# RWKV chunk matrices kept as 64 columns, with products on 64x64 tiles and grams of the diagonal blocks alone

## What is computed

```python
def step(state, inp):
    r_t, d_t, k_t, v_t, kk_t, a_t = inp
    s_a = jnp.einsum('bhvk,bhk->bhv', state, -kk_t)
    state = (state * d_t[:, :, None, :] + s_a[..., None] * (kk_t * a_t)[:, :, None, :]
             + v_t[..., None] * k_t[:, :, None, :])
    return state, jnp.einsum('bhvk,bhk->bhv', state, r_t)
wkv, y = lax.scan(step, wkv0, (rh, dh, kh, vh, kk, ah))
```

## Time and profile before

| | |
|---|---|
| median of 3 runs | 1603.11 us (1602.9 to 1606.72) |
| the profiled execution | 1596.52 us, span 1594.9 us, mean granted TensorE clock 0.972 |
| TensorE products | 1497.1 us busy (94%), 7652 records |
| TensorE weight loads | 784.4 us (49%) |
| VectorE | 585.6 us (37%), 963 instructions |
| ScalarE | 270.2 us (17%) |
| GpSimd (POOL) | 137.2 us (9%) |
| chain that ended last | TensorE 61%, DMA 30%, issue 4%, VectorE 3%, ScalarE 2% |

### The profile page before, as it was taken

How to read it: one execution, slowest core, us unless ns; L and a number is a source line. 1 busy time by engine, 2 the same in 40 slices (tenths; PEclk the granted TensorE clock), 3 DMA queues, 4 the chain that set the end, 5 groups by cost and what they waited for, 6 DMA issues and landing times.

```text
span 1594.9 us, 20792 instructions
## 1 busy us (share of the span) xinstructions
PE 1497.1 (94%) x7652; PEld 784.4 (49%) x7652; DVE 585.6 (37%) x963; ACT 270.2 (17%) x535; POOL 137.2 (9%) x256
## 2 busy tenths in 40 slices
PE   8999989799899888899999999999999999999995
PEld 6877545467788764443344344344334334334431
DVE  2999846823455544312112122121221221211214
ACT  1111523222211112110111111011011011011102
POOL 5332332130110020000000000000000000000000
PEclk9999999899899989899999999999999999999998
DMA  9899997793011063699999999999999999999994
GB/s 337 332 342 345 375 361 253 267 307 118 15 54 53 1 241 122 266 418 429 429 429 428 428 429 429 428 430 428 428 428 429 429 429 427 429 428 429 429 428 188
DMA packets 67886, 534.13 MB, mean 335 GB/s; under 512 B 8587, under 2 KB 9686, under 8 KB 35062
## 3 DMA queue, kind: packets, MB, share of 16 engines
q1 hardware_dynamic: 48774, 471.52, 71.6%
q0 software_dynamic: 8656, 41.97, 7.3%
q10 hardware_dynamic: 10400, 19.92, 3.4%
HBM read 528.92 MB, written 4.46 MB: 334 GB/s over the span
## 4 chain that ended last, share of the span: by engine, by line
PE 61%; DMA 30%; issue 4%; DVE 3%; ACT 2%; POOL 0%; POOLq 0%; SPq 0%; DVEq 0%; ACTq 0%
PE bank L786 58%; DMA projT<-in_w_gate_up 26%; PE bank L787 2%; DMA ring<-in_w_mem_kv 1%; DMA ring<-in_w_in 1%; DMA arena<-in_state_rw_wkv 1%; DMA out_wkv_sample<-arena 1%; ACT arena L1618 0%; DMA ring<-in_cache_sb_v 0%; DVE arena L2288 0%; DMA arena<-in_x_sample 0%; POOLq L459 0%; DVE arena L2377 0%; DVE arena L2394 0%; ACT memT L1889 0%
## 5 line engine op out<-in xcount | busy, mean ns | idle before, releaser
L786 PE MATMUL bank<-arena 128*128 128x128 f32 (+7 forms) x2130 | 326.7, 356 | 12.5 <-DVE arena L2337 3.6
L786 PE MATMUL bank<-ring,memT 128*64 128x512 f32 (+2 forms) x1152 | 283.8, 600 | 10.8 <-ACT memT L1889 8.3
L786 PEld LDWEIGHTS bank<-arena 128*128 128x128 f32 (+4 forms) x2130 | 221.3, 179 | 126.4 <-issue 112.5
L786 PE MATMUL bank<-projT,ring 128*128 128x264 f32 x1056 | 260.1, 402 | 7.5 <-DVE projT L2297 2.7
L2501 DVE TENSOR_SCALAR arena<-bank 128x256 f32<-128x256 f32 x64 | 27.0, 421 | 639.2 <-PE bank L786 639.2
L786 PE MATMUL bank<-projT 128*64 128x512 f32 (+1 forms) x1056 | 232.4, 586 | 9.1 <-DMA projT<-in_w_gate_up 9.1
L786 PE MATMUL bank<-ring,projT 128*64 128x512 f32 x1024 | 230.3, 597 | 0.0
L786 PEld LDWEIGHTS bank<-projT,ring 128*128 128x128 f32 x1056 | 204.1, 198 | 49.9 <-issue 5.2
L786 PEld LDWEIGHTS bank<-ring,memT 128*64 128x64 f32 (+2 forms) x1152 | 85.0, 139 | 156.8 <-issue 138.0
L786 PEld LDWEIGHTS bank<-projT 128*64 128x64 f32 (+1 forms) x1056 | 75.1, 138 | 161.7 <-issue 134.9
L786 PEld LDWEIGHTS bank<-ring,projT 128*64 128x64 f32 x1024 | 69.3, 137 | 147.4 <-issue 147.4
(11 more groups left out here) (272 smaller groups left out, 853.1 us busy)
## 6 DMA issues: line engine op xcount, KB each, us to landing
ring<-in_w_gate_up SPq DMA_DIRECT2D x64, 2048.0 KB, 22.0
projT<-in_w_gate_up SPq DMA_DIRECT2D x64, 2048.0 KB, 24.3
ring<-in_w_down SPq DMA_DIRECT2D x64, 2048.0 KB, 20.4
ring<-in_cache_sb_k SPq DMA_DIRECT2D x64, 256.0 KB, 6.2
ring<-in_cache_sb_k POOLq DMA_DIRECT2D x64, 256.0 KB, 5.9
ring<-in_cache_sb_v SPq DMA_DIRECT2D x64, 256.0 KB, 5.6
ring<-in_cache_sb_v POOLq DMA_DIRECT2D x64, 256.0 KB, 5.4
ring<-in_w_in ACTq DMA_DIRECT2D x7, 2048.0 KB, 14.0
```

Source lines behind the costliest of these rows:

```text
L786: mm = lambda out, l, r, first, last, **k: pe.matmul(out, l, r, start=first, stop=last, **k)
```

## The change

- The matrices of a unit keep 64 columns: partitions 0 to 63 hold chunk 0's block, partitions 64 to 127 chunk 1's. The masks have 64 columns too.
- X, TX, XT, MV and Z become `in_chunks`: eight products of 64x64 tiles with 64 moving columns, one on rows and columns 0 to 63, one on 64 to 127, in turn.
- `grams` takes both head halves together, and only the diagonal blocks: 64x64 tiles on all four positions, into two banks. All of g2 now stands ahead of dS(1).
- RB, RK and the inverse for WT stay 128 wide, block diagonal: RB and RK are zeroed once by POOL (new wait `blocks_zero`), `Tfull` by VectorE, and only their diagonal blocks are written. In level 4 VectorE writes `Tl` (64 columns, for Z) and then `Tfull` in two halves (for WT). Z now waits for `T_last`, not for the bank of XT4.
- VectorE's and ScalarE's operations on these matrices have half the columns; those on RB and RK are twice as many, on 64 partitions each.

```diff
-        lev = [sb(f"lev{i}", [P, P]) for i in range(6)]
+        lev = [sb(f"lev{i}", [P, C]) for i in range(6)]
...
-                g.tensor_tensor(lev[i][:], same[i + 1], lo, ALU.subtract).then_inc(sem("masks"), 1)
-            link(g.tensor_tensor(m_up[:], tri_lt[:], blk[:], ALU.mult))
...
+                for h in halves:
+                    ins = g.tensor_tensor(lev[i][h, :], same[i + 1][h, h], lo[h, h], ALU.subtract)
+                ins.then_inc(sem("masks"), 1)
+            for h in halves:
+                link(g.tensor_tensor(m_up[h, :], tri_lt[h, h], blk[h, h], ALU.mult))
...
+            g.wait_ge(*full_of(("ys", 0)))
+            for a in RBs + RKs:
+                ins = g.memset(a, 0.0)
+            ins.then_inc(sem("blocks_zero"), 1)
             g.wait_ge(sem("out_done"), 16 * n_out)
             g.sem_inc(sem("arena_clear"), 1)
...
+            def grams(n, nm):
...
+                bs = [start((nm, hp) + n) for hp in range(2)]
                 for i, lr in enumerate({"g1": ("BA", "AB"), "g2": ("BR", "KA"), "g3": ("KR",)}[nm]):
                     for tl in range(2):
...
+                        for hp in range(2):
+                            rows = slice(64 * hp, 64 * hp + 64)
+                            for cc, h in enumerate(halves):
+                                cols = slice(tt * P + C * cc, tt * P + C * cc + C)
+                                ins = mm(bs[hp][h, P * i + C * tl:P * i + C * tl + C], hats[lr[0]][rows, 2 * hh + tl, cols],
+                                         hats[lr[1]][rows, 2 * hh + tl, cols], True, True)
...
+            def in_chunks(b, left, right):
+
+                for u in range(4):
+                    for h in halves:
+                        last = mm(b[h, C * u:C * u + C], left(u)[h], right(u)[h], True, True)
+                return last
...
-                    for u in range(4):
-                        last = mm(b[:, u * P:u * P + P], Nm[lv % 2][:, u, :], Tm[:, u, :], True, True)
-                    done(("X", lv) + n, last)
+                    done(("X", lv) + n, in_chunks(b, lambda u: Nm[lv % 2][:, u, :], lambda u: Tm[:, u, :]))
...
+                pe.wait_ge(sem("T_last"), it + 1)
+                b = start(("Z",) + n)
+                done(("Z",) + n, in_chunks(b, lambda j: Tl[:, 2 * (j % 2) + j // 2, :], lambda j: MVs[:, j, :]))
                 gone(pe, ("XT", 4) + n)
...
-                        last = mm(b[64 * hp:64 * hp + 64, P * tl:P * tl + P], tokAB[:, 0, c0:c0 + 64], Tt[:, u, :], True, True)
+                        last = mm(b[64 * hp:64 * hp + 64, P * tl:P * tl + P], tokAB[:, 0, c0:c0 + 64], Tfull[:, u, :], True, True)
...
                 if ahead:
-                    gram(ahead, "g2", 0)
+                    grams(ahead, "g2")
                 state_change(1)
-                if ahead:
-                    gram(ahead, "g2", 1)
...
-                    move(("X", lv) + n, Xm.rearrange("p a b -> p (a b)"), lambda b: b[:, :])
+                    move(("X", lv) + n, Xm.rearrange("p a b -> p (a b)"), lambda b: b[:, 0:256])
...
             v.wait_ge(sem("arena_clear"), 2)
+            v.memset(Tfull, 0.0)
             v.memset(Sb[0], 0.0).then_inc(sem("S_zero"), 1)
...
-                    tt_(RBs[it % 2][:, u], part(b, 0), m2(m_upi), ALU.mult)
+                    for h in halves:
+                        tt_(RBs[it % 2][h, u, h], part(b, 0)[h], m2(m_upi)[h], ALU.mult)
...
+                if it == 0:
+                    v.wait_ge(sem("blocks_zero"), 1)
                 other_products(it)
...
-                    tt_(Tt, Tt, b[:, :].rearrange("p (a b) -> p a b", a=4), ALU.add).then_inc(freed_by(("XT", lv) + n), 1)
+                    if lv < 4:
+                        tt_(Tt, Tt, units(b), ALU.add).then_inc(freed_by(("XT", lv) + n), 1)
+                    else:
+                        tt_(Tl, Tt, units(b), ALU.add).then_inc(sem("T_last"), 1)
+                        for h in halves:
+                            ins = tt_(Tfull[h, :, h], Tt[h], units(b)[h], ALU.add)
+                        ins.then_inc(freed_by(("XT", lv) + n), 1)
```

More of the change, by code:

```diff
@@ L343, in build @@
         tokABs, tokKVs = ([ar(R0 + 1024 * i + 512 * j, 2, 256) for i in range(2)] for j in range(2))
-        Nt, Tm, Tt, Xm, AK = (ar(R0 + 2048 + 512 * i, 4, P) for i in range(5))
+        Nt, Tm, Tt, Xm, AK, Tl = (ar(R0 + (2048, 2304, 2560, 2816, 3072, 3840)[i], 4, C) for i in range(6))
+        Tfull = ar(R0 + 3328, 4, P)
         RBs, RKs = ([ar(R0 + 4608 + 1024 * i + 512 * j, 4, P) for i in range(2)] for j in range(2))
-        Nm = [ar(R0 + 6656 + 512 * i, 4, P) for i in range(2)]
+        Nm = [ar(R0 + 6656 + 512 * i, 4, C) for i in range(2)]
+        last_state = ar(R0 + 6656, 4, P)
         MVs, Zs, Us = (ar(R0 + 7680 + 256 * i, 4, 64) for i in range(3))
@@ L376, in build @@
         moe_slot = [ring[:, 0, :], ring[:, 2, :], proj[:, 0:SLOT], proj[:, SLOT:2 * SLOT], ring[:, 3, :], ring[:, 1, :]]
+        halves = (slice(0, C), slice(C, P))
         gate_at = lambda dt: pT[:, (V0 if dt < 4 else K0 - 4) + dt, :]
@@ L1198, in turned_hats @@
                 done((nm,) + n, last)
[L1200 removed]
+            def grams(n, nm):
                 tt, hh = n
[L1203 to L1205 removed]
+                bs = [start((nm, hp) + n) for hp in range(2)]
                 for i, lr in enumerate({"g1": ("BA", "AB"), "g2": ("BR", "KA"), "g3": ("KR",)}[nm]):
                     for tl in range(2):
[L1208 to L1210 removed]
+                        last = []
+                        for hp in range(2):
[4 more added lines that the diff above has]
+                                         hats[lr[1]][rows, 2 * hh + tl, cols], True, True)
+                            last.append(ins)
+                for hp in range(2):
+                    done((nm, hp) + n, last[hp])
+            def in_chunks(b, left, right):
[3 more added lines that the diff above has]
+                return last
             def group_mean(t):
@@ L1228, in _ @@
             for nm in ("g1", "g2"):
-                for hp in range(2):
-                    gram(RW_PARTS[0], nm, hp)
+                grams(RW_PARTS[0], nm)
             for it, n in enumerate(RW_PARTS):
@@ L1234, in _ @@
                 tokAB, tokKV, RB, RK = (x[it % 2] for x in (tokABs, tokKVs, RBs, RKs))
-                for hp in range(2):
-                    gram(n, "g3", hp)
+                grams(n, "g3")
                 branches(*at_place(it, "start"))
```

54 lines of the change are left out of this document (21 added, 33 removed).

## The result

The changed kernel took 1584.72 us (median of four runs, 1578.9 to 1589.78) against 1603.01 for the kernel before (1598.1 to 1606.72): ratio 0.9887, 95% interval 0.9843 to 0.993. A second set of six runs gave 1581.68 against 1598.92, ratio 0.9873 (0.9836 to 0.9911). It is faster, by 17 to 18 us. The forecast was 1580, a saving of 23.3, with a range of its own of 1574 to 1586.

The account below looks back on a forecast made before the run. TensorE bounds the RWKV stage, DMA the expert stream behind it. Savings of 13.9 (levels), 3.5 and 0.1 (their end), 4.9 (grams) and 0.9 (start) sum to 23.3: 1603.1 to 1579.8 us; own range 1574 to 1586, wider range to 1600.

Parts of the forecast that it names:

- Level: One level of the RWKV stage: 2.93 us instead of 3.80, held by TensorE's products and branches; 0.87 saved.
- The step that counted four whole levels a part: RWKV stage: 0.87 us saved a level, taken for 16 levels over four parts, 13.9 us.
- End of the levels: From the first X4 record to the branches behind WT: 5.01 us instead of 6.16, 1.15 saved; 3.5 in three parts.
- Grams and transition: Between parts: Y starts 1.35 us sooner and g3 saves 0.27, together 1.62 three times, 4.9 us.
- A part: Period of one of the four parts of the RWKV stage: down from 36.4 to 30.1 us.
- The start: First part's grams and VectorE's first masks shrink while the clock is at half: 0.9 us saved, between 0 and 3.
- The fourth part: End of the last part's levels: 0.7 us gain up to XT4 cut by 0.6 more on VectorE, leaving 0.1.
- POOL: Memsets hidden behind a 10.15 us DMA; perhaps 1.5 us more mask work hidden in 3.45 us idle: no cost.
- The rule that spoke against it: X, TX and XT pairs: row tiles can't share a PSUM bank simultaneously; held strictly, tiles run in turn, 1614 us.
- whatever moves the start of the experts moves the end one for one: Behind the RWKV stage: experts wait for every layer ahead, so the whole 23.3 us saving was subtracted from the end time.
- The third rival: TensorE's clock falls inside the RWKV stage: four half-clock levels cost 7.5 us, so 1587; all sixteen near 1611; chance 0.08.
- The expert stream unchanged in length: Expert weights' DMA stream, from 646 us to the end: a sign that its length stays the same.

Follow-up runs that it names:

- the two kernels with the code of before: The unedited kernel before, and the same with five more POOL mask operations (ratio 1.0004): 1052.2 and 1052.4 us from first reciprocal to end.
- The kernel with 13 products: Changed kernel, last eight branch products moved into TensorE's wait in the last part, 13 unread products added before the rank counts: 1572.74 us, ratio 0.9816.
- the same two fillings: Last eight branch products moved into TensorE's wait, 13 unread products before the rank counts: changed kernel 1572.74 us, kernel before 1598.17 us.

## Why the prediction was right, and where it missed

**The sum.** 23.3 was forecast for the stage, and the stage gave 22.5 (149.6 less 127.1).

- *Level*: forecast 2.93, measured 2.90 to 2.91. The dependent chain by itself is 2.40 (forecast 2.49), TensorE with its branches is the bound, the group is 0.46 from first to last start, and two tile records start 7 ns apart (forecast: within 20). VectorE's add 0.42 and ScalarE's copy 0.38 to 0.39, as in the rows of the narrower shapes. The step that counted four whole levels a part was a little generous. From the first TX record to the fourth are three levels, which saved 0.89 each; on the last one's way to X4 0.71 was saved, and ahead of the first TX nothing (5.46 from the branches to TX, where it was 5.44). That is 3.4 a part for the forecast 3.48.
- *End of the levels*: forecast 5.01, measured 5.07 (X4 at 434.10, the branches behind WT at 439.17).
- *Grams and transition*: Y's gain was forecast as 1.35 and is 1.30 (branches behind WT to Y: 7.14 us where it was 8.44); g3's was 0.27 and is 0.26 (448.68 less 446.31, and 0.39 to the branches). VectorE's state holds U(1), as forecast, here for 0.35.
- *A part*: forecast 30.1, measured 30.34. *The start*: forecast 0.9, measured 0.8 (8.78 us from ScalarE's first copy to X0, 413.71 to 422.49; 9.61 before). TensorE even began later: its first product stands 1.23 us behind that copy's start instead of 0.65, with two of ScalarE's copies ahead of it in the chain of waits instead of one. The forecast had no such term. *The fourth part*: forecast 3.6 with its levels, measured 3.5.
- *POOL*: nothing, as forecast: shown for the masks by the run with longer ones, and for the memsets by their end under the transfer.

**The rule that spoke against it.** The Trainium skill, TensorEngine Tiling (Array Packing), Gotcha 1: PSUM Pressure, states that different row tiles cannot access the same PSUM bank simultaneously. Here the pair of each product uses rows 0 to 63 and 64 to 127, writes the partitions of the same halves, and both write one bank; it ran side by side: 2.91 us a level against 4.02 with one tile alone. For tiles that write different partitions of a bank the measurement decides against the rule.

**What was missed.** The sum was taken off "either" time, on the step that whatever moves the start of the experts moves the end one for one. This step failed by a fifth: of the 22.5 us at the reciprocals 17.3 arrived at the end. The third rival looked for a new fall of the clock inside the stage; there was none. But the clock also falls behind the stage, at 546 to 565 us and later in the kernel before, and a shift of the stage moves these falls against the work. I had read the 0.64 of that stretch and used it only as a warning for the stage. Its price is 5.1 us: 22.46 less 5.12 is 17.3, by the second profile 22.35 less 5.65 is 16.7, and the medians say 18.3 and 17.2. With a term of 0 ± 5 us for it the forecast would have had the same centre and an honest reason for its width. As it stands, that both medians (1584.7 and 1581.7) lie in the range of 1574 to 1586 is owed to the stage's terms, which were right, and to some luck, since the range had no room set aside for this cost. "The expert stream unchanged in length" is right within 1.2 us (943.7 against 942.5 from behind the gather on), which is again a fall of the clock, near 1561 us: eight records from 1560.61 on take 3.31 us, and 1.94 in the kernel before.

**What stays open.** Why the falls lie where they lie for a given length of the stage: two profiles of one kernel agree on them (the tails of after, 1057.3 and 1057.9, and of the two kernels with the code of before, 1052.2 and 1052.4), so they go with the kernel more than with the execution, but nothing here lets one work out the position beforehand. The kernel with 13 products, in which the clock rose earlier inside the stage than in the others, was profiled once, so it isn't known whether this repeats. Nor was it tried to shift the changed kernel in several steps to look for its best position.

## What to carry to other kernels

When the matrices have a zero half, products on two 64x64 tiles give most if the tiles alternate in the order of issue (stage 127.1 us; 139.4 with four and four, 151.7 with one tile, 149.6 before); check with one tile alone what the overlap gives, and with the filler work taken out which bound is next. Cut every comparison of two profiles at the marks of the stage that was edited, and read the granted clock behind it: a stretch that wasn't edited can take back a quarter of the gain. If it does, put work that is due anyway, and where there is none a few idle products no longer than the wait, into TensorE's long waits, and count them so that they hardly outlast the wait. Then measure: the same two fillings took 11.1 us off the changed kernel's tail and 0.9 off that of the kernel before.

## What was not expected of the hardware

- The granted clock behind the stage depends on the stage's length: 1.7 us more ahead of the reciprocals made the tail of the kernel before 1057.5 instead of 1052.2 us, and 1.8 us more made that of the changed kernel 1055.6 instead of 1057.3.
- A fall costs most where TensorE is dense (48 records took 14.02 instead of 10.65 us); among products that nobody reads it cost 1.2 us.
- Two 64x64 tiles overlap wholly when they alternate (2.91 us a level), by half when each gets four products in a row (3.46), against 4.02 without overlap. Of eight records in a row on one tile, the fifth had to start before the other tile's first did (0.287 us late); with four in a row it was 0.03.
- A 64x64 product in f32 steps by 0.058 us a record, the value worked out from the load of 64 columns and the streaming of 64, with no allowance for issue.
